# Dense layers of a three-pass fp32r product: three products of 256 columns a chunk into one half of a PSUM bank, instead of one of 512 and one of 256 into two halves

## What is computed

```python
# first block
proj = h @ w_in + b_in                      # 1024 x 5632
merged = sigmoid(gate_r) * (y_rnn @ w_o_rnn) + sigmoid(gate_a) * (y_att @ w_o_attn)
mix = merged @ w_out
x = x + g1 * rmsnorm(mix);  x = x + g2 * rmsnorm(moe_ffn(norm(x)))
# second block, i = 0, 1
def swiglu(h, w_in, w_out):                 # 1024 x 5632, 2816 x 1024
    gate, up = jnp.split(h @ w_in, 2, axis=-1)
    return (jax.nn.silu(gate) * up) @ w_out
h = h + 0.5 * swiglu(rmsnorm(h), ffn1_w_in[i], ffn1_w_out[i])
h = h + mixer_i(rmsnorm(h))                 # conv: 1024 x 3072 and 1024 x 1024; attention: 1024 x 9216 and 1024 x 1024
h = h + 0.5 * swiglu(rmsnorm(h), ffn2_w_in[i], ffn2_w_out[i])
```

## Time and profile before

| | |
|---|---|
| median of 3 runs | 2460.07 us (2459.31 to 2471.74) |
| the profiled execution | 2457.9 us, of which 2456.1 us are its span |
| granted TensorE clock, mean | 0.994 of 2.4 GHz |
| stretch of the first block's mixer | 0 to about 320 us |
| stretch of the experts | about 320 to 1245 us |
| stretch of the second block | about 1254 to 2456 us |

### The profile page before, as it was taken

How to read it: one execution, slowest core, us unless ns; L and a number is a source line. 1 busy time by engine, 2 the same in 40 slices (tenths; PEclk the granted TensorE clock), 3 DMA queues, 4 the chain that set the end, 5 groups by cost and what they waited for, 6 DMA issues and landing times.

```text
span 2456.1 us, 35541 instructions
## 1 busy us (share of the span) xinstructions
PE 2350.5 (96%) x13386; PEld 1623.9 (66%) x13387; DVE 1385.7 (56%) x2592; ACT 1009.2 (41%) x1858; POOL 74.7 (3%) x125
## 2 busy tenths in 40 slices
PE   7999999999999999999989999999999889998999
PEld 4778744444444444444468888888888777776888
DVE  5677733322222232222267769886786677776785
ACT  4656521111111111111155555655654666674653
POOL 0000000000000000000000000000000111001000
PEclk9999999999999999999999999999999999999999
DMA  9764779999999999999965555555555655552553
GB/s 330 266 234 134 292 332 424 425 426 426 426 427 427 426 427 426 427 426 427 425 227 187 173 187 189 189 184 176 190 191 186 180 144 147 150 144 85 182 185 124
DMA packets 277971, 673.67 MB, mean 274 GB/s; under 512 B 8485, under 2 KB 236112, under 8 KB 244961
## 3 DMA queue, kind: packets, MB, share of 16 engines
q1 hardware_dynamic: 274656, 663.60, 71.0%
q0 software_dynamic: 3200, 8.53, 2.0%
HBM read 670.45 MB, written 1.12 MB: 273 GB/s over the span
## 4 chain that ended last, share of the span: by engine, by line
PE 85%; DVE 6%; ACT 5%; issue 3%; SPq 1%; DMA 1%; DVEq 0%; ACTq 0%
PE PS L384 26%; PE PS L1502 18%; PE PS L385 13%; PE PS L1524 9%; PE PS L1489 5%; PE PS L392 4%; PE PS L1476 3%; PE PS L393 2%; DVE WS L334 1%; ACT WS L330 1%; DVE XG L1619 1%; PE PS L2105 1%; PE PS L2120 1%; SPq L302 1%; PE PS L2093 1%
## 5 line engine op out<-in xcount | busy, mean ns | idle before, releaser
L384 PE MATMUL PS<-HN,WS 128*128 128x512 f32 x1952 | 694.3, 400 | 14.0 <-DVE WS L334 9.3
L334 DVE TENSOR_TENSOR WS<-RAW,WS 128x1024 fp32r<-128x1024 f32 (+1 forms) x452 | 540.8, 1205 | 136.1 <-ACT WS L330 131.0
L385 PE MATMUL PS<-HN,WS 128*128 128x256 f32 x1952 | 545.5, 279 | 0.0
L330 ACT ACTIVATE WS<-RAW 128x1024 fp32r<-128x1024 f32 (+1 forms) x452 | 462.9, 1034 | 79.9 <-PE PS L385 69.8
L1502 PE MATMUL PS<-RING,XG 128*64 128x512 f32 x2048 | 446.6, 594 | 11.0 <-DVE XG L1619 11.0
L384 PEld LDWEIGHTS PS<-HN,WS 128*128 128x128 f32 x1952 | 367.9, 188 | 105.4 <-DVE WS L334 12.6
L385 PEld LDWEIGHTS PS<-HN,WS 128*128 128x128 f32 x1952 | 369.0, 189 | 0.3
L1502 PEld LDWEIGHTS PS<-RING,XG 128*64 128x64 f32 x2048 | 149.1, 137 | 294.2 <-issue 293.1
L1625 DVE TENSOR_SCALAR GLU<-PS 128x256 f32<-128x256 f32 x64 | 27.2, 424 | 413.4 <-PE PS L1502 413.4
L384 PE MATMUL PS<-MI,WS 128*128 128x512 f32 x704 | 245.4, 395 | 0.0
L1524 PE MATMUL PS<-RING,AT 128*64 128x512 f32 x1024 | 226.8, 594 | 14.8 <-ACT AT L1398 14.8
(11 more groups left out here) (358 smaller groups left out, 2548.5 us busy)
## 6 DMA issues: line engine op xcount, KB each, us to landing
RING<-in_moe_w SPq DMA_DIRECT2D x192, 2048.0 KB, 21.7
RAW<-in_ffn_w_in SPq DMA_DIRECT2D x88, 1024.0 KB, 5.1
RAW<-in_attn_w_qkv SPq DMA_DIRECT2D x36, 1024.0 KB, 5.1
RAW<-in_ffn_w_out SPq DMA_DIRECT2D x32, 1024.0 KB, 5.0
RAW<-in_w_in SPq DMA_DIRECT2D x22, 1024.0 KB, 5.5
RAW<-in_w_ada SPq DMA_DIRECT2D x18, 1024.0 KB, 8.3
RAW<-in_ffn_w_out SPq DMA_DIRECT2D x16, 768.0 KB, 4.3
RAW<-in_conv_w_in SPq DMA_DIRECT2D x12, 1024.0 KB, 5.1
```

Source lines behind the costliest of these rows:

```text
L330: act_f(split_tile(0, n), raw_tile(n), ACT.Copy).then_inc(hi_done, 1)
L334: vec.tensor_tensor(split_tile(1, n), raw_tile(n), split_tile(0, n).bitcast(f32), ALU.subtract).then_inc(lo_done, 1)
L384: nc.tensor.matmul(both, hi[:, k, :], x2[:, :, kx, :], start=start, stop=False)
L385: ins = nc.tensor.matmul(half, lo[:, k, :], x2[:, 0, kx, :], start=False, stop=stop)
```

## The change

All dense layers are changed at once. A chunk becomes three PE instructions of 256 columns, all into the first half of the bank: `hi` with `x_hi`, `hi` with `x_lo`, `lo` with `x_hi`, each with a weight load of its own (the load of `hi` is issued twice). The second half of each bank is no longer used. A tile leaves by one ACT operation, `take_tile`, that reads the first half and raises `evacuated` itself. `add_half` and the semaphore `half_out` are gone; where `add_half` stood, DVE waits for `evacuated` (`own_sum`). The order of the work is otherwise kept.

```diff
-            both = dense_bank(L, u.tile)[:, :]
-            half = both[:, 0:S]
+            out_tile = tile_bank(L, u.tile)
             start, stop = u.first and k == 0, u.last and k == u.kc - 1
             if not L.tok:
                 hi, lo = split_tile(0, u.n), split_tile(1, u.n)
-                nc.tensor.matmul(both, hi[:, k, :], x2[:, :, kx, :], start=start, stop=False)
-                ins = nc.tensor.matmul(half, lo[:, k, :], x2[:, 0, kx, :], start=False, stop=stop)
+                nc.tensor.matmul(out_tile, hi[:, k, :], x2[:, 0, kx, :], start=start, stop=False)
+                nc.tensor.matmul(out_tile, hi[:, k, :], x2[:, 1, kx, :], start=False, stop=False)
+                ins = nc.tensor.matmul(out_tile, lo[:, k, :], x2[:, 0, kx, :], start=False, stop=stop)
             else:
...
-                nc.tensor.matmul(both, x2[:, 0, kx, x], w2, start=start, stop=False)
-                ins = nc.tensor.matmul(half, x2[:, 1, kx, x], w2[:, 0], start=False, stop=stop)
+                nc.tensor.matmul(out_tile, x2[:, 0, kx, x], w2[:, 0], start=start, stop=False)
+                nc.tensor.matmul(out_tile, x2[:, 0, kx, x], w2[:, 1], start=False, stop=False)
+                ins = nc.tensor.matmul(out_tile, x2[:, 1, kx, x], w2[:, 0], start=False, stop=stop)
...
-    def take_half(act, L, t, dst, func=ACT.Copy, **scaling):
+    def take_tile(act, L, t, dst, func=ACT.Copy, **scaling):
         act.wait_ge(mm_done, L.end[t])
-        act_f(dst, tile_half(L, t), func, **scaling).then_inc(half_out, 1)
-
-    def add_half(dve, L, t, dst, scale=1.0):
-        dve.wait_ge(half_out, L.t0 + t + 1)
-        if isinstance(scale, float) and scale == 1.0:
-            ins = TTN(dst, tile_bank(L, t), dst, ALU.add)
-        else:
-            ins = STT(dst, tile_bank(L, t), scale, dst, ALU.mult, ALU.add)
-        ins.then_inc(evacuated, 1)
+        act_f(dst, tile_bank(L, t), func, **scaling).then_inc(evacuated, 1)
...
             def work_gate(t):
-                add_half(dve, gate, t, GATE[:, t, :])
+                own_sum(dve, gate, t)
                 own_sum(dve, gate, t)
```

More of the change, by code:

```diff
@@ L199, in block_program @@
     hi_done, lo_done = sem("hi_done"), sem("lo_done")
-    mm_done, half_out, evacuated = sem("mm_done"), sem("half_out"), sem("evacuated")
+    mm_done, evacuated = sem("mm_done"), sem("evacuated")
     def cols(w, where=lambda pair: 2 * P * pair):
@@ L388, in chunk_of @@
                 w2 = WS[:, :, :].rearrange("p t (s k n) -> p t s k n", s=SLOTS_W, k=DC)[:, :, s:s + 2, k, :]
-                both = both.rearrange("p (t s n) -> p t s n", t=2, s=2)
-                half = half.rearrange("p (s n) -> p s n", s=2)
+                out_tile = out_tile.rearrange("p (s n) -> p s n", s=2)
                 x = slice(tt * P, (tt + 1) * P)
-                nc.tensor.matmul(both, x2[:, 0, kx, x], w2, start=start, stop=False)
-                ins = nc.tensor.matmul(half, x2[:, 1, kx, x], w2[:, 0], start=False, stop=stop)
+                nc.tensor.matmul(out_tile, x2[:, 0, kx, x], w2[:, 0], start=start, stop=False)
+                nc.tensor.matmul(out_tile, x2[:, 0, kx, x], w2[:, 1], start=False, stop=False)
+                ins = nc.tensor.matmul(out_tile, x2[:, 1, kx, x], w2[:, 0], start=False, stop=stop)
             if k == u.kc - 1:
@@ L702, in work_win @@
                 if Q <= part < K_:
-                    take_half(act, win, t, of(t), ACT.Identity, bias=QB[:, part - Q:part - Q + 1], scale=HD ** -0.5)
+                    take_tile(act, win, t, of(t), ACT.Identity, bias=QB[:, part - Q:part - Q + 1], scale=HD ** -0.5)
                 else:
-                    take_half(act, win, t, of(t), ACT.Identity, bias=col("b_in", part))
+                    take_tile(act, win, t, of(t), ACT.Identity, bias=col("b_in", part))
             def round_merged(t):
@@ L1066, in work_win @@
                 if Q <= WIN_PART[t] < K_:
-                    add_half(dve, win, t, of(t), HD ** -0.5)
+                    own_sum(dve, win, t)
                 else:
-                    add_half(dve, win, t, of(t))
+                    own_sum(dve, win, t)
             def work_wor(t):
-                add_half(dve, wor, t, WT[:, t % 4, :])
+                own_sum(dve, wor, t)
                 if t >= 3:
@@ L1082, in work_woa @@
             def work_woa(t):
-                add_half(dve, woa, t, WT[:, t % 4, :])
+                own_sum(dve, woa, t)
                 if t == 0:
@@ L1881, in work_b @@
             def work_b(t):
-                add_half(dve, cb, t, B[:, t, :])
+                own_sum(dve, cb, t)
                 own_sum(dve, cb, t)
@@ L2057, in work @@
                 if n is None:
-                    take_half(act, qkv, t, v_chunk(t), scale=token_root(t))
+                    take_tile(act, qkv, t, v_chunk(t), scale=token_root(t))
                 else:
@@ L2061, in work @@
                         act.wait_ge(sem("q_normed"), n - 3)
-                    take_half(act, qkv, t, QRAW[n % 4][:, :], scale=token_root(t))
+                    take_tile(act, qkv, t, QRAW[n % 4][:, :], scale=token_root(t))
                 before(t)
@@ L2251, in work @@
                 n = query(t)
-                add_half(dve, qkv, t, v_chunk(t) if n is None else QRAW[n % 4][:, :], token_root(t))
+                own_sum(dve, qkv, t)
                 before(t)
```

26 lines of the change are left out of this document (12 added, 14 removed).

## The result

Median 2489.24 us (2487.41 to 2489.47, four runs) against 2462.29 us for the kernel before (2459.31 to 2471.74, four runs): ratio 1.0104, 95% interval 1.0085 to 1.0123. The profiled execution took 2487.41 us with a span of 2485.6, 29.5 us more than the span before.

The account below looks back on a forecast made before the run. PE was taken to bound the dense stretches, at 3552 times a chunk's pace. From 2457.9 us, -5 for PE and -2 for exits gave 2451 us, forecast as no change; range 2410 to 2510 us.

Parts of the forecast that it names:

- the price of the new chunk: PE, dense layers: three narrow products at 115 ns make 345 against 347, 348 to 350 against 352.5; about -5 us.
- The argument from half clock: PE before 1261 us: 256 and 512 columns take 0.21 and 0.43 us, so no fixed cost in array cycles exists.
- each load and product pair has a cost of its own: Slower rival on PE: 13 and 16.5 ns per added pair, 53 us, 2509 us; or 36 us at 120 ns; chance 0.28.
- The prediction's 93%: PE's weight loads: busy share estimated to grow from 66% by 668 us to 93%, nearly full, yet not over.
- Exits: Tile exits: DVE's dropped addition saves 0.42 to 0.5 us at each of a few exposed waits, -2 us in all.
- The norm's opening: PE's 1.91 us wait at 1462.23 us for a split behind the norm's reciprocal: said to gain nothing.
- The first weights of qkv: PE's wait at 1918.01, whose split stands behind a block's end: said to shorten by the addition's 0.42 to 0.5 us.
- The waits for EN: Attention's largest PE waits, L2209, 18.4 us in twelve: said to gain nothing, as the addition lies before their chain.
- The shared supply: Much slower rival on PE: loads and moving columns share one supply, 43 ns more a chunk, 153 us, about 2609; chance 0.04.
- the floor of 111 ns: Faster rival on PE: the load sets the narrow interval, three take 334 ns, 58 us less, 2398 us; chance 0.11.
- DVE as the bound: Faster rival: DVE was the bound at more edges than seen, -20 us, 2433 us with the -5; chance 0.10.
- the two paces: Dense chunks on PE take 347 or 352.5 ns by stretch; the page doesn't say why, so the choice can't be foreseen.

Follow-up runs that it names:

- the kernel in turns: Kernel before with its two products' order alternating by chunk (wide, narrow, then narrow, wide); same work and sums: 2459.76 us, ratio 0.9986.
- the kernel with halves kept apart: Kernel before with its wide product split in two, the second filling the bank's other half, exit by ACT and DVE as before: 2489.32 us, ratio 1.0115.

## Why the prediction was wrong

**The step that failed** is the price of the new chunk: "So I price all three at the narrow interval: three times 115 ns is 345 in the fast pace, against 347". Three narrow products took 360 ns. The forecast's sum had -5 us for PE in it and came to 2451 us; PE's busy time grew by 34.8 us, and the profiled execution took 2487.41. That this lies inside the stated range is owed to the rival's price at its upper end, and not to the forecast. The total of 347 ns was read rightly; its split between wide and narrow was not. "18 and 8 ns, in proportion to the columns" came from the starts of two unequal products, 231 and 115 ns apart. In streams of equal products, where no split is needed, the same 27 ns are 13.3 and 13.3: 226.7 with 512 columns, 120 with 256. The prediction took the narrow product between wide ones for "exactly the situation that the new chunk has three times". It isn't: a short product's interval hangs on the stream around it, which is the sign of being wrong that the prediction names itself (starts that aren't independent of what follows).

How a mixed stream comes to divide its 27 ns as 18 and 8 is open. A start that is merely late behind a wide product would not explain it, since the kernel in turns has like products two by two, and there too two narrow ones follow each other after 115 ns and two wide ones after 233 (means of the window from 1280 to 1455 us). Its timeline of PE:

```profile
1601.07 0.28 PE L386 MATMUL PS<-HN,WS 128*128 128x256 f32 x1
1601.18 0.28 PE L388 MATMUL PS<-HN,WS 128*128 128x256 f32 x1
1601.30 0.40 PE L389 MATMUL PS<-HN,WS 128*128 128x512 f32 x1
1601.53 0.40 PE L385 MATMUL PS<-HN,WS 128*128 128x512 f32 x1
1601.77 0.28 PE L386 MATMUL PS<-HN,WS 128*128 128x256 f32 x1
```

So an interval read in a mixed stream isn't what the product costs in a stream of its own kind.

**The argument from half clock** failed with it. The rows show that nothing is on top at 1.2 GHz, before and after; "no fixed cost in array cycles exists" does not follow for 2.4 GHz, where the same product of 256 columns has 13.3 ns on top.

**The rival** "each load and product pair has a cost of its own" is what happened. Its largest price, 16.5 ns a pair in the slow stretches, was too high, since a part of those 33 ns comes of the unequal widths and went with them; the price that it named for 120 ns throughout, 14 ns on 1584 chunks and 7 on 1968, is 36 us, and PE's busy time grew by 34.8. The bound of 119 ns from which it decides was the right sign to look for. Its 0.28 was too little beside 0.47: both rested on how 27 ns divide between two products, which the start rows alone could not tell.

**The Trainium skill.** TensorE: Matmul & The Clock Gate, Back-to-back issue gap, gave 131 ns for a pair with 512 columns and, for a product by itself, columns at 2.4 GHz and 2.5 ns. The runs have 226.7 ns a pair, 13.3 over the columns, and do not bear out the first; a product by itself stands in none of these streams, so the second isn't tested here. Perfetto Trace Analysis, Identifying the Most-Contended Engine, takes the busy share of loads, the sum of their durations over the window, for the measure of TensorE's headroom. The prediction's 93% added durations (3552 times 0.188 us) to a busy time in which loads that overlap count once. A load lasts 0.19 us and the next begins 0.12 us later, so the busy time grew by 202.8 us to 73%; added up, the durations of all loads are 2298 us before and 3007 us after, 94% and 121% of the span. By the skill's own measure the loads were thus over the span, which the prediction had as "not over". In the dense stretches the share is full even with overlaps counted once. Windows of all loads (us, busy, count, clock, DMA share, GB/s) of the kernel before:

```profile
1280.00:1455.00 175.00, 151.76 (x991) 1.00 0.57 187
```

of the kernel after:

```profile
1280.00:1455.00 175.00, 175.00 (x1460) 1.00 0.57 186
```

and of the one with three products of 512:

```profile
1280.00:1455.00 175.00, 144.90 (x772) 1.00 0.32 103
```

The measure pointed to the right place. It doesn't price it: with loads at 83% (144.90 of 175) in that last kernel, and no two of them overlapping, each pair still pays the same 13.3 ns.

**The other steps.** Exits: -2 us was said; PE's idle time fell by 5.3, of which the kernel with halves kept apart leaves 0 to 3 for the exits. The norm's opening stayed as said (1.87 us for 1.91). The first weights of qkv gained 1.8 us, more than the addition's 0.42 to 0.5; their wait is now ended by PE's own issue. The waits for EN were to stay and grew by 3.2 us. DVE's busy time fell by 151.9 us and not 168: the durations of its rows, added up, did fall by 166, but rows that overlap count once in busy time. The shared supply (390 ns a chunk), the floor of 111 ns (seen with 64 and with 128 columns, but below the 120 of 256) and DVE as the bound didn't occur. That the choice between the two paces was "the largest thing that I can't foresee" held in its way: the change ended it, and this halved the loss in the stretches that had been slow.

## What to carry to other kernels

Count pairs of load and product, not columns alone: here each whole pair of 256 to 512 columns at 2.4 GHz cost 13.3 ns over them, so cutting 512 columns into two products of 256 adds 6% to them. Price a product by the period of a steady stretch of nothing but such products, never by a gap in a mixed stream, and test a split of such a sum with a kernel in which all are alike. Work removed from an engine that is covered is worth only its edges: 152 us of DVE's bought at most 3 here.

## What the hardware showed that was not expected

- Products of 256, 384 and 512 columns came every 120, 173.3 and 226.7 ns at full clock; at half clock 256 came every 213 ns, with nothing on top.
- 128 columns came every 111 ns at full clock, hardly sooner than 256, and every 213 ns at half clock, as 256 did. In their one run the granted clock was 0.50 for most of the second block, with PE busy throughout the long window: 3140.65 us for fewer columns.
- 32 and 64 stationary columns beside a whole load cost the same inside a tile, 353.3 ns a chunk, and three halves 340.
- Two products of 512 and 256 took 346.7 to 353.3 ns, by stretch and order, two of 384 always 346.7. In turns, two narrow ones in a row came 115 ns apart and two wide ones 233, not the 120 and 226.7 that they take among their like. The kernel before also spread more from run to run (2454.33 to 2469.00 us over 15 runs) than the one after (2487.41 to 2489.47 over four); that its paces change between runs would explain this, but isn't shown, as there is a trace of only one of its runs.
